# Prompt attention turned round: values as weights, turned probabilities moving

## The chip, the cores and the metric

The kernel runs on one core of a Trainium2 chip. The metric is device microseconds from the first to the last instruction of one launch; the median of several runs counts. TensorE multiplies (stationary weights, moving columns), VectorE and ScalarE work elementwise, GpSimd as well, SyncE starts the transfers. Each engine works through its own list in order, and they wait for each other by semaphores.

## What is computed

One layer of a hybrid decoder in fp32: 2064 prompt rows (16 meta and 2048 new) and 8 running sequences of 4 rows. Each layer runs sliding-window attention with sinks beside a gated delta recurrence, merges them by gates, and adds a feed-forward block. The change is in the attention of the prompt:

```
s = einsum('bnqkgd,bnskd->bnkgqs', qb, kband) * (HEAD_DIM ** -0.5)   # block of 128 queries, 256 keys
p = exp(s - m);  p = p / (sum(p) + exp(sink - m))
o = einsum('bnkgqs,bnskd->bnqkgd', p, vband)
h = h + (ga * (oa @ w_oa) + gb * (ob @ w_ob)) @ w_out
```

There are 8 query heads of 64 features, in two groups of four (GQ) for two key and value heads (NKV).

## The kernel before

The prompt is worked in four groups (NG) of four tiles (NT) of 128 rows; group 0 also carries the 48 small rows (16 meta, 32 of the running sequences), called tile "S". Each group runs through stages in written order: input projections (fp32r products, each weight split in a high and a low part: ScalarE casts `wh`, VectorE subtracts to get `wl`, L1628); the convolution blocks j = 0 to 11; the delta recurrence of one tile after another; the z blocks; the output projections; the feed-forward block. All these projections are issued by the helper at L724.

The attention of a tile is laid beside other work in steps. A table names for each part the step k at which every engine's list has it: `IN_CONV` for tile 0 of groups 1 to 3, whose steps are the convolution blocks, `IN_DELTA` for the next tile while the delta recurrence of this one runs, `IN_DELTA_S` beside tile "S". A part exists for both gk = 0 and 1, that is for the first and second four heads; 32 such rounds in all. A round is: scores on TensorE (L887, one head on each half of the rows), mask and maxima on VectorE (L1696, L1664 to L1667), exponentials on ScalarE (L1336), the turn of the 128 x 256 probabilities of four heads by eight transposes (L899), copies of the turned ones out of PSUM to `pTm` by ScalarE (L1350) and VectorE (L1681), and the products with the values (L912). `denominators` gives one over the sum of each row (L1672, L1673).

Within the delta stretch the steps are: k = 3 + 2q after TensorE's first product chain of level q (L1043) and the transposes to X (L1048), k = 4 + 2q after the second (L1056), for q = 0 to 4. L1043 waits for VectorE's Y pass (L1913), which waits for L1056; L1056 waits for ScalarE's copies PT and X (L1429, L1433). k = 13 follows the products L1063 and L1067. `QUARTERS` gives for each k how many quarters of a gate block (six products of 512 columns by L724) TensorE works there, ahead of the attention's part; after every fourth quarter ScalarE casts and VectorE splits the next weight, also ahead of the attention's part. That is at k = 2, 6, 12 and 17. GpSimd masks for level q (L1577) after the first product of level q - 2.

At the end of the attention the rows of `qkv` hold the output with tokens on the partitions. In the z stretch TensorE transposes them (L1138) into PSUM, ScalarE rounds them to `oT[0]`, VectorE takes the rest to `oT[1]` (L1982), and the output projection reads both.

Of the kernel before, what the change touches and what calls it, by code (L numbers as in the profile page):

```python
# [55 lines left out]
assert sum(QUARTERS) * NT == 64  # L56
IN_DELTA = dict(inputs=2, scores=(3, 8), exp=(5, 10), transposes=(6, 11), values=(7, 13))
IN_DELTA_S = dict(inputs=1, scores=(2, 6), exp=(3, 7), transposes=(4, 8), values=(5, 13))
# [23 lines left out]
for _v, _names in {  # L82
# [18 lines left out]
        (0, 4, 4):  # L101
            "oaT_ps ob_hi ob_lo prod_done z_silu",
        (0, 5, 4):
# [6 lines left out]
        (0, 8, 8):  # L110
            "hn_hi hn_lo hsq_done mix_f mix_hi mix_lo pT_rd0 sqc_done sum_ps ysq_done",
        (0, 9, 0):
# [139 lines left out]
def program(nc, d):  # L252
# [130 lines left out]
    for n in """hi_done lo_done unit_started const_in param_in ident_in x_in0 x_in1 x_in2 x_in3 x_inS xT_in rope_in conv_state_in  # L383
        hx_in hxS_in kv_out y_out end_out yS_out s_cache_in s_state_in s_mask_in v_meta_in
        act_step dve_step pool_step sq_done rr_done xR_ps xs_done xh_done xl_done a_ps a_rd ab_rd
        beta_done rope_done conv_ps conv_rd conv_y conv_post tail_done attT_ps att_in sc_ps sc_done pexp_done
        pT_ps pT_rd0 pT_rd1 pv_ps oa_done e_done att_m nat_ps G_ps arg_done dec_done natq_done bt_ps bt_rd kk_ps
        A_done QK_done X_done Y_ps Y_done m_done PT_ps PT_done X_ps X_rd DT_ps XY_done WU_ps WT_rd U_rd WS_ps u_done ob_rd
        QB_zero small_p o_ps dS_ps S_done osq_done orr_done ob_done gate_ps gate_e gate_done z_ps z_silu obT_ps ob_lo oaT_ps
        oT_hi oT_lo prod_done mix_ps mixS_ps mix_rd mix_f mix_hi mix_lo state_out act_g dve_g gate_eS act_pre  # L390
        ob_hi dve_S out_ps h_done hn_hi hn_lo hsq_done hacc_done hsum_ps hpre_done hrr_done hR_ps hR_done
        ff_ps_g ff_ps_u ga_done sg_done hu_done hf_done hid_hi hid_lo down_ps h2_done ysq_done yacc_done sqc_done sum_ps
        gc_ps gc_in sums_in rs_done eg_done ysumS_ps ypreS_done yrrS_done yRS_ps yS_done ysum_ps ypre_done yrr_done yR_ps y_done kwm_done masked_done""".split():
        sem(n)
# [228 lines left out]
    def group(g, first):  # L623
# [90 lines left out]
        def tensor(pe, claim):  # L714
# [176 lines left out]
            def att_transposes(t, gk):  # L891
                r = round_of(t, gk)
                pe.wait_ge(*made("pexp_done", r + 1))
                for q in range(2):
# [7 lines left out]
            def att_values(t, gk):  # L902
# [5 lines left out]
                claim(4, "oa_done", r + 1)  # L908
                for y in range(GQ):
                    ps = slice(HD * (y % NKV), HD * (y % NKV + 1))  # L910
                    for s in range(2):
                        last = nc.tensor.matmul(bank[4][:, HD * y:HD * (y + 1)], pTm[:, 2 * y + s, :], vn[:, s, ps],  # L912
                                                start=s == 0, stop=s == 1)
# [219 lines left out]
            for j in range(NH):  # L1133
                feature_block("z", j, (1, 0)[j % 2], 2, "z_ps", "z_silu", j + 1)
                b = (6, 7)[j % 2]
                claim(b, "oT_lo", (j + 1) * (1 + F))
                for t in range(NT):
                    last = nc.tensor.transpose(bank[b][:, P * t:P * (t + 1)], qkv[:, t + 1, P * j:P * (j + 1)], c("ident"))  # L1138
                last.then_inc(sem("oaT_ps"), 1)
                if j == 0:  # L1140
# [117 lines left out]
        def scalar(act):  # L1258
# [211 lines left out]
            for j in range(NH):  # L1470
# [6 lines left out]
                act.activation(sz[:, CA], bank[(1, 0)[j % 2]][:, 0:WA], ACT.Silu).then_inc(sem("z_silu"), 1)  # L1477
                act.wait_ge(*made("oaT_ps", j + 1))
                act.copy(oT[0][:, j, MAIN], bank[(6, 7)[j % 2]][:]).then_inc(sem("oT_hi"), 1)
                if first:  # L1480
# [125 lines left out]
        def vector(dve):  # L1606
# [68 lines left out]
            def attention_step(t, where, k):  # L1675
                for gk in range(NKV):
                    r = round_of(t, gk)
                    if k == where["transposes"][gk]:
                        denominators(r, GQ)
                        dve.wait_ge(*made("pT_ps", r + 1))  # L1680
                        v_.tensor_copy(pTm[:, 4:8, :], bank[2][:].rearrange("p (a n) -> p a n", a=4)).then_inc(sem("pT_rd1"), 1)  # L1681
                        settle()
                    if k == where["values"][gk]:
                        dve.wait_ge(*made("pv_ps", r + 1))
                        v_.tensor_tensor(qkv[:, t + 1, 256 * gk:256 * (gk + 1)].rearrange("p (a e) -> p a e", a=GQ),
                                         bank[4][:, 0:GQ * HD].rearrange("p (a e) -> p a e", a=GQ),
                                         bc(st[:, 20:20 + GQ], [P, GQ, HD]), ALU.mult).then_inc(sem("oa_done"), 1)
                    if k == where["scores"][gk]:
# [288 lines left out]
            for j in range(NH):  # L1977
                lo_until("z", j)
                dve.wait_ge(*made("oT_hi", (1 + F) * (j + 1)))
                if first:  # L1980
                    v_.tensor_tensor(oT[1][:, j, SM], qkv[:, 0, NS * j:NS * (j + 1)], oT[0][:, j, SM].bitcast(F32), ALU.subtract).then_inc(sem("oT_lo"), 1)
                v_.tensor_tensor(oT[1][:, j, MAIN], bank[(6, 7)[j % 2]][:], oT[0][:, j, MAIN].bitcast(F32), ALU.subtract).then_inc(sem("oT_lo"), 1)  # L1982
                dve.wait_ge(*made("z_silu", j + 1))
# [243 lines left out]
```

## Time and profile before

| | us |
|---|---|
| median of 3 runs (3611.22 to 3614.88) | 3612.71 |
| the profiled execution's own time | 3614.01 |
| its span | 3612.0 |
| TensorE busy (matmuls) | 3495.0 |
| VectorE busy | 1764.9 |
| ScalarE busy | 1290.5 |
| GpSimd busy | 305.7 |
| mean granted TensorE clock | 0.979 of full |

Busy time is the union of an engine's instructions. A fp32 product shows as two matmul instructions in the trace, a transpose as one. The start of a matmul row is when it enters; the rows merge instructions of one line that follow each other, with their number behind the x.

### The profile page before, as it was taken

The numbers are of one execution on the slowest core, as the hardware profiler recorded it, in microseconds if no ns is written. First come the engines' busy times: TensorE is split into PE (matmuls) and PEld (weight loads), VectorE is DVE, ScalarE is ACT, GpSimd is POOL, SyncE is SP. The second block draws the span as 40 slices with busy tenths as digits, with TensorE's granted clock in tenths as the row PEclk, the third lists the DMA queues.
The fourth block names the chain that finished last, engine by engine and source line by source line (L and its number), as shares of the span: only waits on it lengthen the run. The fifth ranks groups of instructions, "written<-read, shape, count | busy, mean of one in ns | idle before, by whom it ended". The sixth has DMA issues, their size and how long they took to land. (4 is left out here: it accounts for less than half of the span.)

```text
span 3612.0 us, 48790 instructions
## 1 busy us (share of the span) xinstructions
PE 3495.0 (97%) x19972; PEld 3032.7 (84%) x19972; DVE 1764.9 (49%) x3003; ACT 1290.5 (36%) x2302; POOL 305.7 (8%) x289
## 2 busy tenths in 40 slices
PE   7979999999999999999999999999999999999998
PEld 6868889999998888888878888888888888888886
DVE  3834334543436654554345744554344754454343
ACT  3313334321224544432224544432223544432222
POOL 2211110000003111000001211000000311000000
PEclk9969989999999999999999999999999999999999
DMA  4101102322233211333333211232324211233322
GB/s 170 60 19 53 32 24 71 105 86 87 88 129 106 63 36 42 105 100 94 94 134 119 71 37 42 71 117 96 97 90 164 80 38 36 68 109 103 95 93 85
DMA packets 88541, 298.63 MB, mean 83 GB/s; under 512 B 12272, under 2 KB 14272, under 8 KB 87536
## 3 DMA queue, kind: packets, MB, share of 16 engines
q1 hardware_dynamic: 88320, 295.51, 25.5%
q8 instruction: 160, 2.62, 0.3%
q14 instruction: 61, 0.50, 0.0%
HBM read 283.86 MB, written 12.62 MB: 82 GB/s over the span
## 5 line engine op out<-in xcount | busy, mean ns | idle before, releaser
L724 PE MATMUL bank<-hnT,wh 128*128 128x512 f32 (+1 forms) x3520 | 931.4, 352 | 0.0
L1628 DVE TENSOR_TENSOR wl<-raw,wh 128x1024 fp32r<-128x1024 f32 x480 | 594.7, 1239 | 642.8 <-ACT wh L1274 641.6
L724 PE MATMUL bank<-xnT,wh 128*128 128x512 f32 (+2 forms) x2560 | 736.6, 374 | 12.6 <-DVE d_dT L1879 9.9
L724 PEld LDWEIGHTS bank<-hnT,wh 128*128 128x128 f32 x3520 | 619.4, 188 | 91.4 <-issue 0.2
L1274 ACT CAST wh<-raw 128x1024 fp32r<-128x1024 f32 x480 | 500.5, 1043 | 391.3 <-PE bank L724 331.4
L724 PE MATMUL bank<-hnT,wl 128*128 128x512 f32 (+1 forms) x1760 | 622.2, 354 | 0.0
L724 PEld LDWEIGHTS bank<-xnT,wh 128*128 128x128 f32 x2560 | 448.7, 193 | 79.1 <-DVE d_dT L1879 11.2
L724 PE MATMUL bank<-hid,wh 128*128 128x512 f32 (+1 forms) x1760 | 468.3, 354 | 4.4 <-DVE wl L1628 3.2
L724 PE MATMUL bank<-xnT,wl 128*128 128x512 f32 (+2 forms) x1280 | 467.6, 366 | 0.0
L724 PEld LDWEIGHTS bank<-hnT,wl 128*128 128x128 f32 x1760 | 330.6, 188 | 45.8
L724 PEld LDWEIGHTS bank<-hid,wh 128*128 128x128 f32 x1760 | 309.6, 188 | 52.4 <-DVE wl L1628 5.2
L724 PE MATMUL bank<-hid,wl 128*128 128x512 f32 (+1 forms) x880 | 310.8, 353 | 0.0
L724 PEld LDWEIGHTS bank<-xnT,wl 128*128 128x128 f32 x1280 | 246.3, 192 | 39.8
L1519 ACT CAST hid<-hf 128x512 fp32r<-128x512 f32 (+1 forms) x88 | 55.5, 630 | 419.5 <-DVE hf L2080 419.5
L724 PEld LDWEIGHTS bank<-hid,wl 128*128 128x128 f32 x880 | 165.5, 188 | 23.9
L724 PE MATMUL bank<-oT,wh 128*128 128x512 f32 (+1 forms) x640 | 169.4, 353 | 4.4 <-DVE oT L1982 3.2
L724 PE MATMUL bank<-mixT,wh 128*128 128x512 f32 (+1 forms) x640 | 169.4, 352 | 1.9 <-DVE mixT L2012 1.9
L1516 ACT ACTIVATE sg<-sg 128x512 f32<-128x512 f32 (+1 forms) x88 | 56.5, 642 | 318.9 <-DVE sg L2068 318.9
L724 PE MATMUL bank<-wh,xnT 128*128 128x512 f32 (+1 forms) x544 | 138.1, 342 | 16.9 <-DVE wl L1628 16.9
L1577 POOL TENSOR_TENSOR d_m<-d_dA,cm 128x512 f32<-128x512 f32 (+1 forms) x83 | 119.8, 1451 | 364.1 <-PE bank L1043 214.2
L502 POOL TENSOR_SCALAR rr<-ss 128x1 f32<-128x1 f32 (+3 forms) x34 | 6.6, 193 | 1523.6 <-ACT xr L508 1028.9
L1913 DVE TENSOR_TENSOR Y<-Y,bank 128x512 f32<-128x512 f32 (+1 forms) x83 | 56.0, 675 | 161.2 <-PE bank L1056 161.2
(296 smaller groups left out, 4429.7 us busy)
## 6 DMA issues: line engine op xcount, KB each, us to landing
raw<-in_wstream SPq DMA_DIRECT2D x472, 512.0 KB, 3.5
xr<-in_x_prompt SPq DMA_DIRECT2D x16, 512.0 KB, 5.6
xT<-in_xT SPq DMA_DIRECT2D x4, 2048.0 KB, 12.0
hT<-in_xT SPq DMA_DIRECT2D x4, 2048.0 KB, 9.1
out_yp_out<-hT SPq DMA_DIRECT2D x16, 512.0 KB, 3.0
raw<-in_wstream SPq DMA_DIRECT2D x8, 528.0 KB, 3.3
Sb<-in_state_delta SPq DMA_DIRECT2D x1, 2048.0 KB, 10.4
out_ds_out<-Sb SPq DMA_DIRECT2D x1, 2048.0 KB, 6.3
```

The lines of the kernel that those rows point to most:

```text
L502: pool_link(pool, nc.gpsimd.tensor_scalar(dst, src, mul, EPS, ALU.mult, ALU.add))
L724: ins = nc.tensor.matmul(*a, **k)
L1274: act.copy(wh[n % HL][:, 0:m], raw[:, n % RAW, 0:m]).then_inc(sem("hi_done"), 1)
L1516: act.activation(sg[j % 2][:, live], sg[j % 2][:, live], ACT.Silu).then_inc(sem("sg_done"), 1)
L1519: act.copy(hid[0][:, jj, live], hf[j % 2][:, live]).then_inc(sem("hid_hi"), 1)
L1577: nc.gpsimd.tensor_tensor(q4[f"m{q % 2}"][0:n, :, 0:n], q4["dA"][0:n, :, 0:n], bh(c(f"lm{l}")[0:n, 0:n], [n, NH, n]), ALU.mult).then_inc(s ...
L1628: v_.tensor_tensor(wl[n % HL][:, 0:m], raw[:, n % RAW, 0:m], wh[n % HL][:, 0:m].bitcast(F32), ALU.subtract).then_inc(sem("lo_done"), 1)
L1913: v_.tensor_tensor(Y[0:n, :, 0:n], Y[0:n, :, 0:n], bank[3][0:n, 0:NH * n].rearrange("p (h n) -> p h n", h=NH), ALU.subtract).then_inc(sem( ...
```

## The change

The turn of the probabilities stays. The products with the values change sides: before, the turned probabilities of a head, one half of its keys at a time, are the weights and 64 columns of values move, eight products a round; after, the values of a kv head (64 columns) are the weights, and the turned probabilities of its two heads move, 256 columns, four products a round. The two kv heads write to the lower and upper half of the PSUM partitions, that is to the two halves of TensorE's columns. The output thus has features on its partitions. Its rows can then no longer be divided by their sums afterwards, so VectorE multiplies the probabilities (128 x 1024) by the reciprocals ahead of the turn, and TensorE's turn waits for that (`att_p`) and no longer for the exponentials. The transposes of the z stretch go away, ScalarE and VectorE read `qkv` there. In `IN_DELTA` the turn moves from steps 6 and 11 to 7 and 12, and the values of gk = 0 from 7 to 8. `IN_CONV` and `IN_DELTA_S` keep their steps.

```diff
-IN_DELTA = dict(inputs=2, scores=(3, 8), exp=(5, 10), transposes=(6, 11), values=(7, 13))
+IN_DELTA = dict(inputs=2, scores=(3, 8), exp=(5, 10), transposes=(7, 12), values=(8, 13))
             def att_transposes(t, gk):
                 r = round_of(t, gk)
-                pe.wait_ge(*made("pexp_done", r + 1))
+                pe.wait_ge(*made("att_p", 2 * t + gk + 1))
...
                 claim(4, "oa_done", r + 1)
-                for y in range(GQ):
-                    ps = slice(HD * (y % NKV), HD * (y % NKV + 1))
-                    for s in range(2):
-                        last = nc.tensor.matmul(bank[4][:, HD * y:HD * (y + 1)], pTm[:, 2 * y + s, :], vn[:, s, ps],
+                turned = pTm[:].rearrange("p (x y) n -> p x y n", x=2)
+                for s in range(2):
+                    for half in range(NKV):
+                        ps = slice(HD * half, HD * (half + 1))
+                        last = nc.tensor.matmul(bank[4][ps, 0:2 * P], vn[:, s, ps], turned[:, :, 2 * half + s, :],
                                                 start=s == 0, stop=s == 1)
...
                 feature_block("z", j, (1, 0)[j % 2], 2, "z_ps", "z_silu", j + 1)
-                b = (6, 7)[j % 2]
-                claim(b, "oT_lo", (j + 1) * (1 + F))
-                for t in range(NT):
-                    last = nc.tensor.transpose(bank[b][:, P * t:P * (t + 1)], qkv[:, t + 1, P * j:P * (j + 1)], c("ident"))
-                last.then_inc(sem("oaT_ps"), 1)
...
-                act.wait_ge(*made("oaT_ps", j + 1))
-                act.copy(oT[0][:, j, MAIN], bank[(6, 7)[j % 2]][:]).then_inc(sem("oT_hi"), 1)
+                if j == 0:
+                    act.wait_ge(*made("oa_done", round_of(NT - 1, NKV - 1) + 1))
+                act.copy(oT[0][:, j, MAIN].rearrange("p (t n) -> p t n", t=NT), qkv[:, 1:, P * j:P * (j + 1)]).then_inc(sem("oT_hi"), 1)
...
                         denominators(r, GQ)
+                        settle()
+                        v_.tensor_tensor(sc[:], sc[:], bc(st[:, 20:20 + GQ], [P, GQ, 2 * P]), ALU.mult).then_inc(sem("att_p"), 1)
                         dve.wait_ge(*made("pT_ps", r + 1))
...
                         dve.wait_ge(*made("pv_ps", r + 1))
-                        v_.tensor_tensor(qkv[:, t + 1, 256 * gk:256 * (gk + 1)].rearrange("p (a e) -> p a e", a=GQ),
-                                         bank[4][:, 0:GQ * HD].rearrange("p (a e) -> p a e", a=GQ),
-                                         bc(st[:, 20:20 + GQ], [P, GQ, HD]), ALU.mult).then_inc(sem("oa_done"), 1)
+                        v_.tensor_copy(qkv[:, t + 1, 2 * P * gk:2 * P * (gk + 1)], bank[4][:, 0:2 * P]).then_inc(sem("oa_done"), 1)
```

The order of TensorE in the delta stretch of the last group's third tile, from k = 9 to k = 13, before (`PT` and `X` are the recurrence's tiles, `sc` the probabilities, `pTm` the turned ones, `vn` the values, L724 on `xnT` the gate's quarters):

```order
L724 MATMUL bank0<-xnT0_80,wl1_78 128x512
L1043 MATMUL bank5<-Y_159,d_m0_153 128x128 [waits PT_done,XY_done,m_done]
L1048 MATMUL bank6<-cm_49,Y_159 128x128 [waits X_rd]
L899 MATMUL bank1<-cm_49,sc_116 128x128 [waits sc_done,pexp_done]
...
L1056 MATMUL bank3<-PT_160,X_158 128x128 [waits XY_done,X_rd,PT_done]
L724 MATMUL bank0<-xnT0_80,wh1_75 128x512
...
L1063 MATMUL bank5<-Y_159,d_kb_146 128x128 [waits PT_done,XY_done]
L1067 MATMUL bank6<-d_bv_148,Y_159 128x128 [waits X_rd]
L912 MATMUL bank4<-vn_54,pTm_117 128x64 [waits oa_done,pT_rd1,pT_rd0]
L1108 MATMUL bank1<-S_52,d_WQ_157 128x128 [waits S_done,pT_rd0,WT_rd]
```

The same place in the changed kernel (its lines behind the values are one higher):

```order
L724 MATMUL bank0<-xnT0_80,wl1_78 128x512
L1044 MATMUL bank5<-Y_159,d_m0_153 128x128 [waits PT_done,XY_done,m_done]
L1049 MATMUL bank6<-cm_49,Y_159 128x128 [waits X_rd]
L1057 MATMUL bank3<-PT_160,X_158 128x128 [waits XY_done,X_rd,PT_done]
L724 MATMUL bank0<-xnT0_80,wh1_75 128x512
...
L899 MATMUL bank1<-cm_49,sc_116 128x128 [waits sc_done,att_p]
...
L1064 MATMUL bank5<-Y_159,d_kb_146 128x128 [waits PT_done,XY_done]
L1068 MATMUL bank6<-d_bv_148,Y_159 128x128 [waits X_rd]
L913 MATMUL bank4<-pTm_117,vn_54 64x256 [waits oa_done,pT_rd1,pT_rd0]
L1109 MATMUL bank1<-S_52,d_WQ_157 128x128 [waits S_done,pT_rd0,WT_rd]
```

The turn stood between L1048 and L1056 and now stands behind the quarter that follows it.

VectorE's order at the same place, k = 11 to 13, before (`st` holds row sums and reciprocals, `wl` is the weight split):

```order
L1672 TENSOR_TENSOR st_68<-st_68 128x4 [waits pexp_done,dve_step,XY_done]
L1673 RECIPROCAL st_68<-st_68 128x4 [waits dve_step]
L1681 COPY pTm_117<-bank2 128x512 [waits pT_ps]
L1913 TENSOR_TENSOR Y_159<-Y_159,bank3 128x512 [waits Y_done,DT_ps,dve_step]
L1628 TENSOR_TENSOR wl0_77<-raw_73,wh0_74 128x1024 [waits hi_done,dve_step,XY_done]
L1685 TENSOR_TENSOR qkv_111<-bank4,st_68 128x256 [waits pv_ps]
```

And in the changed kernel (its lines stand one to three lower):

```order
L1910 TENSOR_TENSOR Y_159<-Y_159,bank3 128x512 [waits DT_ps,Y_done,dve_step,XY_done]
L1625 TENSOR_TENSOR wl0_77<-raw_73,wh0_74 128x1024 [waits hi_done,dve_step,XY_done]
L1669 TENSOR_TENSOR st_68<-st_68 128x4 [waits pexp_done]
L1670 RECIPROCAL st_68<-st_68 128x4 [waits dve_step]
L1678 TENSOR_TENSOR sc_116<-sc_116,st_68 128x1024 [waits dve_step]
L1680 COPY pTm_117<-bank2 128x512 [waits pT_ps]
L1684 COPY qkv_111<-bank4 128x256 [waits pv_ps,dve_step]
```

The reciprocals stood ahead of the Y pass and the weight split, and now stand behind both, with the multiplication of the probabilities after them.

VectorE's order at block j = 6 of the last group's convolution stretch in the changed kernel (`cy` are the taps):

```order
L1625 TENSOR_TENSOR wl2_79<-raw_73,wh2_76 128x1024 [waits hi_done]
L1824 COPY pre0_136<-tail_55 128x3 [waits conv_rd,conv_post]
L1825 COPY tail_55<-pre0_136 128x3 [waits dve_step]
L1768 TENSOR_SCALAR cy0_138<-pre0_136,pr_50 128x512
L1770 SCALAR_TENSOR_TENSOR cy0_138<-pre0_136,pr_50,cy0_138 128x512 [waits dve_step] x3
L1669 TENSOR_TENSOR st_68<-st_68 128x4 [waits pexp_done]
L1670 RECIPROCAL st_68<-st_68 128x4 [waits dve_step]
L1678 TENSOR_TENSOR sc_116<-sc_116,st_68 128x1024 [waits dve_step]
L1680 COPY pTm_117<-bank2 128x512 [waits pT_ps]
```

Nothing moved there; the multiplication is added behind the taps of the block, and TensorE's turn, which follows its own block j = 6, now waits for it.

## Rows read from the trace of the kernel before

**Rows 1.** The page, busy time and share of the span, instructions.

```profile
PE 3495.0 (97%) x19972; PEld 3032.7 (84%) x19972; DVE 1764.9 (49%) x3003; ACT 1290.5 (36%) x2302; POOL 305.7 (8%) x289
```

**Rows 2.** Timeline, TensorE, convolution stretch of group 3: start, us, line, operands.

```profile
2849.96 1.09 PE L899 MATMUL bank<-cm,sc 128*128 128x128 f32 x8
...
2856.42 0.95 PE L985 MATMUL bank<-cm,sqc 128*128 128x1 f32 x8
...
2866.68 1.07 PE L899 MATMUL bank<-cm,sc 128*128 128x128 f32 x8
```

**Rows 3.** Timeline, ScalarE's cast and VectorE, the same stretch.

```profile
2849.81 1.03 ACT L1274 CAST wh<-raw 128x1024 fp32r<-128x1024 f32 x1
...
2850.88 1.23 DVE L1628 TENSOR_TENSOR wl<-raw,wh 128x1024 fp32r<-128x1024 f32 x1 [3.18 <-ACT wh L1274]
...
2855.24 0.18 DVE L1673 RECIPROCAL st<-st 128x4 f32<-128x4 f32 x1
...
2857.31 0.17 DVE L1827 COPY pre<-tail 128x3 f32<-128x3 f32 x1 [0.18 <-ACT pre L1362]
...
2870.56 0.18 DVE L1673 RECIPROCAL st<-st 128x4 f32<-128x4 f32 x1
```

**Rows 4.** Timeline, TensorE (PEld: its weight loads), delta stretch of group 3.

```profile
3028.10 1.04 PE L899 MATMUL bank<-cm,sc 128*128 128x128 f32 x8
...
3031.68 1.89 PE L912 MATMUL bank<-vn,pTm 128*128 128x64 f32 x16
3033.41 1.11 PE L1056 MATMUL bank<-PT,X 128*128 128x128 f32 x8
3034.45 1.13 PE L887 MATMUL bank<-kT,qTt 64*128 64x256 f32 x8
3035.51 0.97 PEld L1043 LDWEIGHTS bank<-Y,d_m 128*128 128x128 f32 x8 [0.33 <-issue]
...
3040.61 1.05 PE L1043 MATMUL bank<-Y,d_m 128*128 128x128 f32 x8
...
3042.87 1.13 PE L1056 MATMUL bank<-PT,X 128*128 128x128 f32 x8
...
3045.23 1.05 PE L1063 MATMUL bank<-Y,d_kb 128*128 128x128 f32 x8
```

**Rows 5.** Timeline, VectorE, the same tile.

```profile
3028.39 1.22 DVE L1628 TENSOR_TENSOR wl<-raw,wh 128x1024 fp32r<-128x1024 f32 x1 [0.63 <-ACT wh L1274]
3029.72 0.18 DVE L1673 RECIPROCAL st<-st 128x4 f32<-128x4 f32 x1
...
3044.10 0.69 DVE L1913 TENSOR_TENSOR Y<-Y,bank 128x512 f32<-128x512 f32 x1 [0.40 <-PE bank L1056]
...
3044.82 1.23 DVE L1628 TENSOR_TENSOR wl<-raw,wh 128x1024 fp32r<-128x1024 f32 x1
```

**Rows 6.** Timeline, TensorE, the small rows' scores on column strips of 32.

```profile
110.73 0.65 PE L849 MATMUL bank<-kcT,QB 128*32 128x128 f32 x8
```

**Rows 7.** Timeline, VectorE's X pass of the last tile.

```profile
3069.60 1.67 DVE L1897 TENSOR_TENSOR X<-cm,X 128x512 f32<-128x512 f32 x1
```

**Rows 8.** GpSimd's mask products, whole run: min/median/max ns, first and last start.

```profile
L1577 POOL TENSOR_TENSOR d_m<-d_dA,cm x83: 591/1301/1800, 197.5 to 3084.9; 128x512 f32<-128x512 f32 x80, 48x192 f32<-48x192 f32 x3
```

**Rows 9.** Timeline, TensorE, delta stretch of the last tile, no attention beside it.

```profile
3093.39 1.05 PE L1043 MATMUL bank<-Y,d_m 128*128 128x128 f32 x8
...
3095.65 1.13 PE L1056 MATMUL bank<-PT,X 128*128 128x128 f32 x8 [0.77 <-ACT PT L1429]
```

**Rows 10.** TensorE's waits: us in total, times, longest.

```profile
PE bank L724 <- DVE oT L1982: 3.2, 3, 1.1
```

**Rows 11.** Stretches: length, busy PE, PEld, DVE, ACT, POOL, clock, DMA share, GB/s.

```profile
2891.00:2893.40 2.40, 0.23 (x2) 0.01 (x1) 2.33 (x6) 0.66 (x2) 0.00 (x0) 1.00 0.00 0
2893.40:2896.00 2.60, 2.60 (x13) 2.46 (x14) 0.55 (x1) 2.57 (x5) 0.00 (x0) 0.54 0.03 6
2896.00:2898.00 2.00, 2.00 (x14) 2.00 (x14) 0.78 (x3) 2.00 (x8) 0.00 (x0) 0.74 0.00 0
```

More of the change, by code:

```diff
@@ L101 @@
         (0, 4, 4):
-            "oaT_ps ob_hi ob_lo prod_done z_silu",
+            "ob_hi ob_lo prod_done z_silu",
         (0, 5, 4):
@@ L110 @@
         (0, 8, 8):
-            "hn_hi hn_lo hsq_done mix_f mix_hi mix_lo pT_rd0 sqc_done sum_ps ysq_done",
+            "att_p hn_hi hn_lo hsq_done mix_f mix_hi mix_lo pT_rd0 sqc_done sum_ps ysq_done",
         (0, 9, 0):
@@ L388, in program @@
         A_done QK_done X_done Y_ps Y_done m_done PT_ps PT_done X_ps X_rd DT_ps XY_done WU_ps WT_rd U_rd WS_ps u_done ob_rd
-        QB_zero small_p o_ps dS_ps S_done osq_done orr_done ob_done gate_ps gate_e gate_done z_ps z_silu obT_ps ob_lo oaT_ps
+        QB_zero small_p att_p o_ps dS_ps S_done osq_done orr_done ob_done gate_ps gate_e gate_done z_ps z_silu obT_ps ob_lo
         oT_hi oT_lo prod_done mix_ps mixS_ps mix_rd mix_f mix_hi mix_lo state_out act_g dve_g gate_eS act_pre
@@ L1981, in vector @@
                     v_.tensor_tensor(oT[1][:, j, SM], qkv[:, 0, NS * j:NS * (j + 1)], oT[0][:, j, SM].bitcast(F32), ALU.subtract).then_inc(sem("oT_lo"), 1)
-                v_.tensor_tensor(oT[1][:, j, MAIN], bank[(6, 7)[j % 2]][:], oT[0][:, j, MAIN].bitcast(F32), ALU.subtract).then_inc(sem("oT_lo"), 1)
+                v_.tensor_tensor(oT[1][:, j, MAIN].rearrange("p (t n) -> p t n", t=NT), qkv[:, 1:, P * j:P * (j + 1)],
+                                 oT[0][:, j, MAIN].bitcast(F32).rearrange("p (t n) -> p t n", t=NT), ALU.subtract).then_inc(sem("oT_lo"), 1)
                 dve.wait_ge(*made("z_silu", j + 1))
```

## The prediction

> **What bounds the kernel now.** I read the page first: TensorE is busy for 3495.0 us of the 3612.0 us span, so almost nothing can be given to it without lengthening the run, and what is taken off it shortens the run unless a wait takes its place [rows 1]. Next I read the timeline of the stretches that hold the change. In the convolution stretch of groups 1 to 3 the reader is to see that TensorE turns the probabilities at 2849.96 and 2866.68 with no idle time before it, straight behind a convolution block [rows 2]. VectorE is far behind it there: the reciprocal of that round ends at 2855.42 and that of the second at 2870.74 [rows 3]. Nobody minds now, since turned probabilities are not yet scaled. In the delta stretch each instruction of TensorE starts as the last one's slot ends, through both rounds [rows 4], while VectorE works in bursts a few us behind it [rows 5].
>
> **Rate of each operation.** Eight turns of 128 columns take 1.04 us, the last one 0.27 of it, so one starts every 0.11 us and the eight hold TensorE for 0.87 us [rows 4]. The 16 instructions of today's value products (two for each of eight) hold it from 3031.68 to 3033.41, 1.73 us [rows 4]. The new ones are four products of 256 columns, eight instructions. No row has just that form; two come near. The scores are also eight instructions of 256 columns, on row halves, and take 1.13 us [rows 4]: one starts every 0.11 us although each has twice the columns of a turn, so two halves run side by side. Column strips do so too: eight products of 128 columns on four strips of 32 columns, all 128 rows, took 0.65 us at half clock [rows 6], where a start every 0.22 us (the turns' rate at half clock) would need over 1.5. So I price the new values like the scores: a slot of 1.06 us. This holds a toll: weight loads behind the scores begin only at 3035.51, 0.33 us late with nothing awaited, and the slot in front of them (3033.41 to 3034.45) is 1.04 us where eight starts of 0.11 would be 0.87 [rows 4]; with 0.2 for the entry at places where none was paid, a round saves 1.73 - 1.06 = 0.67 us at gk = 0 and 0.48 at gk = 1. The bound on the other side: halves one after the other double the spacing, 7 x 0.22 + 0.38 = 1.9 us, which saves nothing.
>
> The Trainium skill speaks against the halves. TensorE: Matmul & The Clock Gate, Part 3, says that a weight load overlaps a product in flight only where the row groups differ, and two column halves have the same rows. By the strips' row the trace disagrees [rows 6], and I go by the row; by the rule the values would stay at some 1.8 us, and that is the third rival below.
>
> **The pass that is added.** VectorE now multiplies the 128 x 1024 probabilities, and TensorE's turn waits for that (att_p) and not for the exponentials. The nearest row with as many elements and both operands in SBUF is the weight split, 1.23 us [rows 5]; I take 1.22, and 0.07 for the semaphore.
>
> *Convolution stretch, groups 1 to 3.* At gk = 0 the chain is: last exponential, ScalarE's cast, weight split, the block's taps, sum, reciprocal, ending at 2855.42 [rows 3]; scaled at 2856.68, turned from 2856.75. TensorE would have gone at 2849.96 [rows 2]. Behind its waiting turn stand the next convolution block and all after it, so 6.8 us are lost. At gk = 1 VectorE's chain hangs on the end of the next block (the copy at 2857.31 waits for it), which moves along. From that block's end (2856.42) to the reciprocal's end are 14.32 us, plus 1.22, 0.04 and 0.07 makes 15.65; today the turn starts 10.26 after it [rows 2, 3]. That is 5.4 more. Minus 0.48 for the values: 11.7 us a group, **35 us** for three. The three groups run the same tables, so I count the one shown three times.
>
> *Delta stretch, gk = 0, turn moved from k = 6 to 7* (nine tiles in groups 1 to 3). Take the rows' tile. The product chain of k = 7 begins at 3028.10, where the turn was, so TensorE would turn at 3031.68 - 0.87 = 3030.81. VectorE ends the split at 3029.62 and the reciprocal at 3029.90 [rows 5]. GpSimd is in between: its mask product, 1.3 us [rows 8], is released by the end of that product chain (1.06 us long), and so asks at 3029.2. VectorE and GpSimd do not read and write together here: an X pass of 512 columns took 1.67 us beside it where the Y pass of that size takes 0.69 [rows 5, 7]. Which is first when the split ends no row shows; I let GpSimd win at 3029.6, to 3030.9; scaled at 3032.2, so TensorE waits 1.4 us. If VectorE wins, it waits 0.4. Less 0.67: **+0.73 us** a tile, bounds -0.3 and +1.1 (sum and reciprocal behind GpSimd too).
>
> *gk = 1, turn moved from k = 11 to 12.* Today the turn at k = 11 costs nothing. From L1043 at 3040.61 to L1056 at 3042.87 are 2.26 us with a turn between them; in the last tile, which has none, from 3093.39 to 3095.65 are 2.26 us too, with 0.77 of waiting for ScalarE's copies [rows 4, 9]. Moved, the turn leaves that wait behind and costs its full 0.87 at k = 12. There it waits also: VectorE passes Y (from 3044.10), then the split that k = 12 begins with (3044.82 to 3046.05), sum and reciprocal to 3046.4, scaling to 3047.7 [rows 5]. TensorE is ready at 3045.23, where L1063 starts [rows 4]: 2.5 us of waiting. Sum 0.87 + 2.5 - 0.48 = **+2.9 us**. A tile is 3.6, nine tiles **32 us**.
>
> *Group 0* holds the other eight rounds. Products of the 48 small rows stand around them or the clock is halved, so the waits are covered or the faster values weigh more; bounded by eight savings of 0.6 (-5) and eight waits of 0.9 net (+7) I take 0.
>
> *z stretch.* 64 turns go, at 0.11 each 7.0 us. The last four of each group were cover: TensorE waits there for oT already [rows 10], and the chain from z over ScalarE to VectorE is as long as before; 4 x 0.45 come back. **-5 us.** Copies and subtractions from SBUF cost their engines what they cost from PSUM and nobody waits for them longer.
>
> **The clock.** After TensorE stood for 2.2 us (busy 0.23 of 2.40) its granted clock was 0.54 and 0.74 of full in the next 2.6 and 2.0 us, the lower of its two levels for most of it [rows 11]: 2.6 x 0.46 + 2.0 x 0.26 = 1.7 us lost. Six waits of 5 to 7 us will each bring such a fall, at 1.7 to 3.4 us, I take 2.5: 15 us. The nine of 2.5 us are just beyond that row's; half of them at 1.7 is 7 us. **+22 us.**
>
> **Sum.** 35 + 32 + 0 - 5 + 22 = +84 us on the profiled execution's own 3614.0 us. The median of the runs shown is 1.3 us below it, so 3612.7 + 84 = 3697 us.
>
> **Rivals.** (a) *Everything hides, faster*: VectorE's scaled tile is there when TensorE comes. Then 32 values save some 0.57 each (18), z gives 5, and only the moved turns cost (9 x 0.87 = 8): 3598 us. It decides where VectorE reaches the round at least 1.6 us ahead of TensorE; against it stands that in the rows VectorE's reciprocal comes 5.5 and 4.1 us after the turn [rows 2, 3]. Chance 0.04. (b) *The waits come but the clock holds*: 3675 us. For it, most waits in the delta stretch are short; against it [rows 11]. Chance 0.2. (c) *The halves don't run side by side*: about 29 values that count cost 0.75 more, 22 us: 3719. Chance 0.12. (d) *The stage's order hides the waits of the delta stretch alone* (GpSimd never in the way and the split done early): 3697 - 32 - 7 = 3658. Chance 0.06. The forecast keeps 0.57, and 0.01 is left for no change.
>
> **Range.** From 3660, which takes in (b) with GpSimd losing the port, to 3728, which takes in (c) and falls of the clock at their upper price. Within 0.2% (7 us) of before is about what a measurement can't tell from no change. Only (a) is faster. Faster 0.04, same 0.01, slower 0.95.
>
> **What would show it.** In the profile after: TensorE's row of turns (L899) waits for VectorE's scaling in the convolution stretch of groups 1 to 3, near 6.8 and 5.4 us, six times; some 1.4 and 2.5 us in nine tiles; L1057 (L1056 today) waits some 0.8 us for ScalarE's copies in nine more places; the new values take about 1.1 us for eight instructions; the scaling takes 1.2 us; PEclk dips in the slices of the three convolution stretches. What would make me wrong: a scaling that is much faster or slower than the split, column halves in turn, or a clock that doesn't fall.

## The result and the profile after

The changed kernel takes 3696.13 us (median of 4 runs, 3692.91 to 3698.36), the kernel before 3612.41 beside it (4 runs, 3611.22 to 3614.88): ratio 1.0229, 95% interval 1.0213 to 1.0245. The change makes the kernel slower by 2.3%, and 3697 was forecast. The span of the profiled execution is 3696.4 us, 84.4 more than before.

The page's busy times and its row of granted clocks, to be held beside [rows 1]:

```profile
PE 3495.9 (95%) x19652; PEld 3005.1 (81%) x19652; DVE 1816.2 (49%) x3035; ACT 1290.7 (35%) x2302; POOL 307.7 (8%) x289
...
PEclk9869999999999999999999899999999999999999
```

TensorE has 320 instructions fewer and the same busy time: products ran at half clock. All that the span grew by is idle. VectorE's 51 us more are no reason in themselves, since it is half idle in either kernel. TensorE's waits show where its idle time is (us in total, times, longest):

```profile
PE bank L899 <- DVE sc L1678: 80.4, 26, 6.8
...
PE bank L1057 <- ACT PT L1425: 15.5, 21, 0.8
...
PE bank L724 <- DVE oT L1979: 6.3, 4, 1.7
```

Before, the turn waited for VectorE nowhere. The turns' rows on TensorE's timeline in group 3: the convolution stretch (first two), then the three delta tiles with attention beside them:

```profile
2911.23 1.97 PE L899 MATMUL bank<-cm,sc 128*128 128x128 f32 x8 [6.73 <-DVE sc L1678]
2936.11 1.97 PE L899 MATMUL bank<-cm,sc 128*128 128x128 f32 x8 [6.06 <-DVE sc L1678]
2989.77 1.09 PE L899 MATMUL bank<-cm,sc 128*128 128x128 f32 x8 [1.32 <-DVE sc L1678]
3006.02 1.97 PE L899 MATMUL bank<-cm,sc 128*128 128x128 f32 x8 [2.38 <-DVE sc L1678]
3051.87 1.09 PE L899 MATMUL bank<-cm,sc 128*128 128x128 f32 x8 [1.32 <-DVE sc L1678]
3068.50 1.09 PE L899 MATMUL bank<-cm,sc 128*128 128x128 f32 x8 [2.72 <-DVE sc L1678]
3112.75 1.09 PE L899 MATMUL bank<-cm,sc 128*128 128x128 f32 x8 [1.33 <-DVE sc L1678]
3129.01 1.97 PE L899 MATMUL bank<-cm,sc 128*128 128x128 f32 x8 [2.35 <-DVE sc L1678]
```

The same work that took 1.04 to 1.09 us takes 1.97 where the granted clock has fallen to the lower level. The stretch around the first wait, with the columns of [rows 11]:

```profile
2907.00:2910.00 3.00, 0.00 (x0) 0.00 (x0) 2.82 (x7) 1.38 (x3) 0.00 (x0) 0.50 0.58 178
2910.00:2914.00 4.00, 2.77 (x11) 2.58 (x12) 1.87 (x2) 0.77 (x2) 0.00 (x0) 0.50 0.00 0
2914.00:2917.00 3.00, 3.00 (x9) 2.32 (x8) 1.23 (x1) 0.77 (x1) 0.00 (x0) 0.50 0.00 0
```

VectorE at that place. Its taps (L1770) end at 2909.63; the sum, the reciprocal and the multiplication are queued behind them:

```profile
2907.30 2.33 DVE L1770 SCALAR_TENSOR_TENSOR cy<-pre,pr,cy 128x512 f32<-128x512 f32 x3
2909.55 0.15 DVE L1669 TENSOR_TENSOR st<-st 128x4 f32<-128x4 f32 x1
2909.74 0.18 DVE L1670 RECIPROCAL st<-st 128x4 f32<-128x4 f32 x1
2909.95 1.23 DVE L1678 TENSOR_TENSOR sc<-sc,st 128x1024 f32<-128x1024 f32 x1
```

**By stage.** To compare stages of two executions I take starts on TensorE's timeline: the first product of k = 13 in a delta tile (L1063, after it L1064) and the first output product that reads oT. The last tile's pair before, and then after:

```profile
3098.00 1.06 PE L1063 MATMUL bank<-Y,d_kb 128*128 128x128 f32 x8
...
3138.69 0.70 PE L724 MATMUL bank<-oT,wh 128*128 128x512 f32 x2 [1.06 <-DVE oT L1982]
```

```profile
3183.70 1.05 PE L1064 MATMUL bank<-Y,d_kb 128*128 128x128 f32 x8
...
3223.10 0.71 PE L724 MATMUL bank<-oT,wh 128*128 128x512 f32 x2 [1.53 <-DVE oT L1979]
```

The stretch between them is 40.69 us before and 39.40 after. The same subtraction for every group gives the table. The second row holds the stages of output, feed-forward, projections and convolution and one delta tile with attention; the third holds two such tiles and one without.

| stretch, groups 0 to 3 or 1 to 3 | before | after | difference |
|---|---|---|---|
| z stretch, groups 0 to 3 | 47.5, 40.7, 40.7, 40.7 | 46.2, 39.4, 39.4, 39.4 | -5.2 |
| first oT product to the first delta tile of the next group | 679.6, 623.7, 622.9 | 697.4, 644.9, 645.1 | +61.2 |
| three further delta tiles | 166.8, 166.4, 166.4 | 176.3, 175.6, 175.9 | +28.2 |
| start to the last delta tile of group 0 | 543.3 | 543.5 | +0.2 |

The sum is +84.4, the whole growth of the span. Six attention tiles cost 28.2, 4.7 each; with three more of them taken off the second row, 47 us are the convolution stretches'.

### The profile page after: what moved, and what is told of

Read it like the earlier page. It is cut to its first block and busy times, and to the rows that moved or that the text cites. A ratio compares the mean times of both kernels' runs of the same rounds, so it can differ in the third digit from the quotient of the medians.

```text
span 3696.4 us, 48182 instructions
## 1 busy us (share of the span) xinstructions
PE 3495.9 (95%) x19652; PEld 3005.1 (81%) x19652; DVE 1816.2 (49%) x3035; ACT 1290.7 (35%) x2302; POOL 307.7 (8%) x289
## 5 line engine op out<-in xcount | busy, mean ns | idle before, releaser
L724 PE MATMUL bank<-hnT,wh 128*128 128x512 f32 (+1 forms) x3520 | 931.4, 352 | 0.0
L724 PE MATMUL bank<-xnT,wh 128*128 128x512 f32 (+2 forms) x2560 | 745.2, 377 | 12.6 <-DVE d_dT L1876 9.9
L724 PEld LDWEIGHTS bank<-hnT,wh 128*128 128x128 f32 x3520 | 619.4, 188 | 91.4 <-issue 0.2
L724 PE MATMUL bank<-hnT,wl 128*128 128x512 f32 (+1 forms) x1760 | 622.2, 354 | 0.0
L724 PEld LDWEIGHTS bank<-xnT,wh 128*128 128x128 f32 x2560 | 455.5, 196 | 81.7 <-DVE d_dT L1876 11.2
L724 PE MATMUL bank<-xnT,wl 128*128 128x512 f32 (+2 forms) x1280 | 471.5, 369 | 0.0
L724 PE MATMUL bank<-hid,wh 128*128 128x512 f32 (+1 forms) x1760 | 468.1, 354 | 2.9 <-DVE wl L1625 2.7
L724 PEld LDWEIGHTS bank<-hnT,wl 128*128 128x128 f32 x1760 | 330.6, 188 | 45.8
L724 PEld LDWEIGHTS bank<-hid,wh 128*128 128x128 f32 x1760 | 309.6, 188 | 50.7 <-DVE wl L1625 4.4
L724 PE MATMUL bank<-hid,wl 128*128 128x512 f32 (+1 forms) x880 | 310.8, 353 | 0.0
L724 PEld LDWEIGHTS bank<-xnT,wl 128*128 128x128 f32 x1280 | 249.5, 195 | 40.4
L724 PEld LDWEIGHTS bank<-hid,wl 128*128 128x128 f32 x880 | 165.5, 188 | 24.0
L724 PE MATMUL bank<-oT,wh 128*128 128x512 f32 (+1 forms) x640 | 169.4, 353 | 6.3 <-DVE oT L1979 6.3
L724 PE MATMUL bank<-mixT,wh 128*128 128x512 f32 (+1 forms) x640 | 169.4, 352 | 1.9 <-DVE mixT L2010 1.9
L724 PE MATMUL bank<-wh,xnT 128*128 128x512 f32 (+1 forms) x544 | 139.2, 344 | 16.9 <-DVE wl L1625 16.9
```

The lines of the kernel that those rows point to most:

```text
L724: ins = nc.tensor.matmul(*a, **k)
```

## The experiments

All ratios are to the kernel before, run beside each experiment on the same chip; its medians there were 3613.1 to 3615.1 us. Differences in us between an experiment and the changed kernel are differences of ratios times 3613, and each ratio is known to some 0.0015, so such a difference is good to about 6 to 8 us; smaller ones need the stages.

**1. Without the multiplication.** A copy of one column stands in its place and the turn waits for the exponentials again; the attention's output stays undivided by its row sums.

```diff
-                        v_.tensor_tensor(sc[:], sc[:], bc(st[:, 20:20 + GQ], [P, GQ, 2 * P]), ALU.mult).then_inc(sem("att_p"), 1)
+                        v_.tensor_copy(st[:, 40:41], st[:, 16:17]).then_inc(sem("att_p"), 1)
...
-                pe.wait_ge(*made("att_p", 2 * t + gk + 1))
+                pe.wait_ge(*made("pexp_done", r + 1))
```

> The changed kernel without VectorE's multiplication; the turn waits for the exponentials again, as before the change (the attention output stays undivided by its row sums). My theory (the whole loss is that TensorE waits for VectorE's scaling, with the clock falls that follow): all waits of the turn go, the rest of the change is a gain: about 3597 us, at most 3604, with no wait over 1 us before a turn in groups 1 to 3. Rival (the moved turns or the new products themselves cost): it stays above the 3612 us of before, by up to 8 us for the turns that leave an idle place of 0.8 us behind.

It took 3596.48 us, ratio 0.9953 (0.9938 to 0.9968). The scaling with all that hangs on it is worth 100 us, and the rest of the change alone would be a gain of 17. TensorE's wait list has no row of L899 left, while the wait left behind by the moved turn stays as in the changed kernel:

```profile
PE bank L1057 <- ACT PT L1425: 15.5, 21, 0.8
```

**2. The old table.** The turn and values of the delta stretch at the steps of the kernel before:

```diff
-IN_DELTA = dict(inputs=2, scores=(3, 8), exp=(5, 10), transposes=(7, 12), values=(8, 13))
+IN_DELTA = dict(inputs=2, scores=(3, 8), exp=(5, 10), transposes=(6, 11), values=(7, 13))
```

> The changed kernel with the old steps (turns at 6 and 11, values at 7 and 13). My theory by the rows: at step 6 the turn waits 3.1 us (now 1.3 at step 7), at step 11 some 0.3 us and fills the wait for ScalarE's copies (now 2.35 + 0.77), so a tile gains about 1.1 us and nine tiles 10 us: 3686 us. Rival (the move of the steps was needed and hides waits): slower than the changed kernel's 3696, by up to 16 us if step 11 waits as long as step 12 does.

It took 3686.77 us, ratio 1.0206 (1.0189 to 1.0223). By the medians the moved table costs about 8 us; the intervals alone allow no more than that it does not help. The stages say more: three further tiles take 173.5, 171.9 and 173.9 us where the changed kernel has 176.3, 175.6 and 175.9, and that of experiment 4, with the steps of the changed one, 174.9 to 175.2. The move thus costs 0.9 to 1.4 us for each tile with attention. TensorE's timeline in the last such tile shows why: the turn of gk = 0 waits 2.95, that of gk = 1 not at all, and L1057 behind it does not wait either.

```profile
3101.17 1.10 PE L899 MATMUL bank<-cm,sc 128*128 128x128 f32 x8 [2.95 <-DVE sc L1678]
...
3116.39 1.09 PE L899 MATMUL bank<-cm,sc 128*128 128x128 f32 x8
3117.32 1.06 PE L1057 MATMUL bank<-PT,X 128*128 128x128 f32 x8
```

At k = 11 the reciprocal and the multiplication stand ahead of the Y pass and the split; moved to k = 12 they stand behind both, as the orders ahead of the prediction show.

**3. Both products on one column half.** The halves one after the other on the lower 64 columns; the features of the upper half are not computed.

```diff
-                for s in range(2):
-                    for half in range(NKV):
-                        ps = slice(HD * half, HD * (half + 1))
-                        last = nc.tensor.matmul(bank[4][ps, 0:2 * P], vn[:, s, ps], turned[:, :, 2 * half + s, :],
+                for half in range(NKV):
+                    ps = slice(HD * half, HD * (half + 1))
+                    for s in range(2):
+                        last = nc.tensor.matmul(bank[4][0:HD, 2 * P * half:2 * P * (half + 1)], vn[:, s, ps], turned[:, :, 2 * half + s, :],
```

> The changed kernel with both kv heads' products on the lower column half, one after the other (the upper half of the attention output isn't computed). My theory (column halves run side by side): the eight instructions take about 1.9 us and not 1.08, 27 rounds count, +24 us: 3720 us. Rival (weight loads don't overlap on halves with the same rows, so the halves never ran side by side; 1.08 us is what eight such instructions take anyway): no change, 3696.

It took 3717.71 us, ratio 1.0289 (1.0274 to 1.0305). TensorE's timeline: the eight instructions take 1.93 us, and their successor starts 1.86 after them.

```profile
3069.43 1.93 PE L913 MATMUL bank<-pTm,vn 128*64 128x256 f32 x8
3071.29 1.13 PE L887 MATMUL bank<-kT,qTt 64*128 64x256 f32 x8
```

In the changed kernel they hold it for 1.02:

```profile
3114.67 1.08 PE L913 MATMUL bank<-pTm,vn 128*64 128x256 f32 x8
3115.69 1.13 PE L887 MATMUL bank<-kT,qTt 64*128 64x256 f32 x8
```

So halves of the columns do run side by side. The Trainium skill (TensorE: Matmul & The Clock Gate, Part 3) ties the overlap of weight loads to different row groups. The prediction read from it that column halves would take turns; the same Part also lists a speedup for three column tiles side by side. All four products here have the same rows, and the measurement decides against that reading.

**4. Order of the halves.** The changed kernel's products with the loop over the halves outside:

```diff
-                for s in range(2):
-                    for half in range(NKV):
+                for half in range(NKV):
+                    for s in range(2):
```

> The changed kernel with the loop over the kv heads outside that over the key halves: both products of the lower column half come first, then both of the upper half, instead of by turns. If neighbours in order must lie on different column halves to overlap, and the queue looks only one ahead, two of four products run alone: the eight instructions of L913 take about 1.5 us instead of 1.1, and the time is some 12 us longer, 3708. If the column halves overlap whatever the order: 1.1 us and 3696.

It took 3694.87 us, ratio 1.0227 (1.0210 to 1.0244), and the eight take 1.09:

```profile
3065.86 1.09 PE L913 MATMUL bank<-pTm,vn 128*64 128x256 f32 x8
3066.88 1.16 PE L1109 MATMUL bank<-S,d_WQ 128*128 128x128 f32 x8
```

The products need not alternate between the halves to overlap. The rival of this run falls.

**5. TensorE kept busy through the waits.** 24 products of 512 columns with an unused result ahead of each of the six turns in the convolution stretches, so that the clock is changed and not the moment at which the scaled tile is there:

```diff
+                if t == 0 and not first:
+                    claim(7, "pT_ps", r + 1)
+                    for _ in range(24):
+                        nc.tensor.matmul(bank[7][:], xnT[0][:, 0, NS:NS + P], xnT[0][:, 1, MAIN], start=True, stop=True)
```

> The changed kernel with 24 unused products of 512 columns (5.5 us) on TensorE ahead of each of the six turns in the convolution stretches of groups 1 to 3, where it waits for 6.8 and 6.1 us anyway. My theory (the falls of the granted clock behind these waits cost 2 to 3 us each): the wait shrinks to about 1 us, the clock stays at its upper level there, and the time falls by about 14 us to 3682. Rival (the clock costs nothing there, only the wait does): 3696, and PEclk rises without effect.

It took 3682.8 us, ratio 1.0196 (1.0181 to 1.0211), some 12 to 13 us less than the changed kernel. TensorE's timeline in group 3, where the turn (here L903) comes 7.69 us after L990 as it came 7.68 after L986 in the changed kernel, but at full clock, and the stretch around it:

```profile
2894.28 0.95 PE L990 MATMUL bank<-cm,sqc 128*128 128x1 f32 x8
2895.09 5.84 PE L896 MATMUL bank<-xnT 128*128 128x512 f32 x24
2901.97 1.09 PE L903 MATMUL bank<-cm,sc 128*128 128x128 f32 x8 [1.04 <-DVE sc L1682]
```

```profile
2900.00:2905.00 5.00, 3.96 (x21) 3.03 (x21) 2.80 (x6) 1.53 (x2) 0.00 (x0) 1.00 0.04 15
```

These six falls are gone, but others with them, so the total alone does not give their price. In the delta tiles the clock falls in three places in place of six, though the waits there are as long as before. The turn that ran at half clock at 3006.02 in the changed kernel is here:

```profile
2991.62 1.09 PE L903 MATMUL bank<-cm,sc 128*128 128x128 f32 x8 [2.35 <-DVE sc L1682]
```

And at the start of each delta stretch, where the changed kernel has a fall and the kernel before has one in two of three groups ([rows 11]), this one has none. In group 3 the fall of the changed kernel is the first row, and the second is what TensorE waits for here:

```profile
2963.00:2969.00 6.00, 4.48 (x25) 4.22 (x25) 2.69 (x8) 5.10 (x12) 0.00 (x0) 0.72 0.01 3
```

```profile
2957.57 0.66 PE L1035 MATMUL bank<-cm,X 128*128 128x128 f32 x4 [1.47 <-DVE X L1898]
```

Where the clock falls at that place, this wait for VectorE's X is 0.2 us or none; where it doesn't, 1.5, in each of the kernels before, after and here. A fall there thus costs next to nothing.

By stage, of the two profiled executions: from the first turn of a convolution stretch to k = 13 of the first delta tile are 90.6 us in every group here, 94.5, 96.5 and 96.6 in the changed kernel, together 15.8 more. About 2 of them are falls in a delta tile (1.6 each, two of which begin just ahead of the mark) and 0.6 those at the start of the delta stretches. That leaves 13 us for the six falls behind the waits for the scaled tile, 2.2 each. The three falls that are gone from the delta tiles are worth 5 more, and 3 us came back where nothing was changed: 16.0 between these two executions, 12 to 13 by the ratios.

**6. The multiplication earlier in the delta stretch.** A hook at the head of a step on VectorE, ahead of the weight split; the turn of gk = 1 goes back to k = 11:

```diff
+IN_DELTA = dict(inputs=2, ..., transposes=(7, 11), values=(8, 13), scale=(6, 11), late=(-1, -1))
...
+            def attention_scale(t, where, k):
+                for gk in range(NKV):
+                    if k == where["scale"][gk]:
+                        denominators(round_of(t, gk), GQ)
+                        settle()
+                        v_.tensor_tensor(sc[:], sc[:], bc(st[:, 20:20 + GQ], [P, GQ, 2 * P]), ALU.mult).then_inc(sem("att_p"), 1)
...
             def beside(t, k):
+                if after(t) is not None:
+                    attention_scale(after(t), IN_DELTA_S if t == "S" else IN_DELTA, k)
```

> The changed kernel with the reciprocals and the multiplication of the probabilities moved one step ahead on VectorE in the delta stretch (k = 6 and 11, ahead of the weight split of that step), and the turn of gk = 1 at k = 11; the convolution stretch stays. Theory (the wait of the turn is the price, and it stands where VectorE reaches the multiplication too late): the waits of L899 of 1.3 and 2.3 us in nine tiles vanish, and so do most of the clock falls of the delta stretch; the hole of L1057 is filled again by the turn of gk = 1. 9 x 4.2 = 38 and some 8 of clock less: about 3650 us. Rival (VectorE's work is only shifted: the multiplication of 1.22 us now delays the weight split or the Y pass, on which TensorE waits instead): 3680 to 3697, with the waits of L724 or L1044 on VectorE up by what L899 loses.

It took 3639.01 us, ratio 1.0076 (1.0061 to 1.0091): 55 us gained where 46 were expected. By stage, the three further tiles of group 3 take 163.1 us, 12.8 less than in the changed kernel and even 3.3 less than before. A tile with attention is 1.7 us shorter than before; the faster values give 1.15 of it, and the runs do not show where the rest comes from. VectorE in the last tile with attention:

```profile
3055.57 1.23 DVE L1677 TENSOR_TENSOR sc<-sc,st 128x1024 f32<-128x1024 f32 x1
3056.71 2.32 DVE L1625 TENSOR_TENSOR wl<-raw,wh 128x1024 fp32r<-128x1024 f32 x1
3059.26 0.69 DVE L1688 COPY pTm<-bank 128x512 f32<-128x512 f32 x1 [0.22 <-PE bank L899]
...
3067.33 1.22 DVE L1677 TENSOR_TENSOR sc<-sc,st 128x1024 f32<-128x1024 f32 x1
```

```profile
3058.18 1.03 PE L899 MATMUL bank<-cm,sc 128*128 128x128 f32 x8
3059.05 1.06 PE L1057 MATMUL bank<-PT,X 128*128 128x128 f32 x8
```

The split has moved behind the multiplication and, beside GpSimd's mask product (from 3056.61), takes 2.32 us; no row of TensorE waits longer for it. The rival, that the pass only shifts the wait to the split or Y, falls.

**7. The multiplication earlier in the convolution stretch.** The same hook at the head of blocks j = 6 and 8, ahead of the weight split and the taps:

```diff
+IN_CONV = dict(inputs=4, scores=(5, 7), exp=(5, 7), transposes=(6, 8), values=(7, 9), scale=(6, 8), late=(-1, -1))
...
+                if not first:
+                    attention_scale(0, IN_CONV, j)
```

> The changed kernel with the multiplication at the head of blocks j = 6 and 8 on VectorE, ahead of the weight split and the taps of the block; the delta stretch stays. Theory (the six waits of 6.8 and 6.1 us are the taps and the split, queued ahead of the multiplication): they fall to under 2 us each, some 28 us less, and the six clock falls of the convolution stretch with them, another 13 to 16: about 3653 us. Rival (the weight split now comes late to the next block): waits of L724 on wl rise by 1.2 us a turn, so some 7 us come back: 3660 to 3665. Rival that the clock falls come from another cause than the wait: they stay, 3668.

It took 3655.72 us, ratio 1.0120 (1.0105 to 1.0135): 39 us gained. TensorE's turns in group 3:

```profile
2881.84 1.09 PE L899 MATMUL bank<-cm,sc 128*128 128x128 f32 x8 [1.62 <-DVE sc L1677]
2900.38 1.09 PE L899 MATMUL bank<-cm,sc 128*128 128x128 f32 x8 [0.96 <-DVE sc L1677]
```

and two stretches, behind the first and around the second:

```profile
2882.00:2886.00 4.00, 4.00 (x17) 3.31 (x17) 3.86 (x8) 3.51 (x5) 0.00 (x0) 0.64 0.38 133
...
2898.00:2902.00 4.00, 3.04 (x22) 2.74 (x21) 3.20 (x7) 3.97 (x8) 0.00 (x0) 1.00 0.00 0
```

The waits are nearly gone. The rival that the weight split would then come late to the next block falls: TensorE waits for `wl` 20.3 us where the changed kernel has 19.6, not the 7 more that it asked for. The clock still fell behind the wait of 1.62 us, in all three groups, and not behind that of 0.96, so not all of the clock's share came back. That fits the 4 us short of the expected 43, a shortfall that the ratios alone could not tell from none.

**8. Both moves.**

> Both moves together: all 24 multiplications of groups 1 to 3 and of the delta stretch ahead of the weight split of their step. If the waits and their clock falls are all of the price, the two gains add: 3696 - 45 - 43 = about 3608, near the kernel before (3613) or below it. If VectorE's added 1.22 us a round moves elsewhere: 3640 or more.

It took 3603.44 us (7 runs, 3600.93 to 3605.83), ratio 0.9972 (0.9961 to 0.9983): faster than the kernel before by 0.3%, and the gains add (55 and 39, together 93). What TensorE still waits for at the turns:

```profile
PE bank L899 <- DVE sc L1686: 8.4, 2, 4.3
PE bank L899 <- DVE sc L1677: 8.0, 6, 1.8
```

These are the two of tile "S", which I did not move, and six of the convolution stretch; they explain that 7 us are missing to the kernel without any multiplication. By stage this one is 9.4 us longer in the second row and 2.6 in group 0, and 5.4 shorter in the further delta tiles, where the other has the wait at L1057.

**9. The old value products.** The eight products of 64 columns in the changed kernel; the output then has its tokens on the partitions, so what the output projection reads is not the layer's attention.

```diff
+                for y in range(GQ):
+                    ps = slice(HD * (y % NKV), HD * (y % NKV + 1))
+                    for s in range(2):
+                        last = nc.tensor.matmul(bank[4][:, HD * y:HD * (y + 1)], pTm[:, 2 * y + s, :], vn[:, s, ps],
```

> The changed kernel with the eight products of 64 columns of the kernel before in place of the four of 256; all else is as in the changed kernel, and the output of the attention is then laid out with the tokens on the partitions, so the values that the output projection reads are not the layer's. Theory (the new products save 0.67 us in gk = 0 and 0.48 in gk = 1): 3696 + 16 x 0.67 + 16 x 0.48 = 3714 us, between 3709 and 3722. Rival (the new ones save nothing, because something else sets the time there): 3696.

It took 3714.18 us, ratio 1.0273 (1.0256 to 1.0290), 16 us more than the changed kernel. Turning the products round is a gain of 16 us, near the 18 that the slots gave.

**10. The z transposes back,** with their output unused:

```diff
+                b = (6, 7)[j % 2]
+                claim(b, "oT_lo", (j + 1) * (1 + F))
+                for t in range(NT):
+                    nc.tensor.transpose(bank[b][:, P * t:P * (t + 1)], qkv[:, t + 1, P * j:P * (j + 1)], c("ident"))
```

> The changed kernel with the sixteen transposes a group issued again in the z stretch into the same banks, their output unused. Theory: the transposes took 7.0 us of TensorE's path, of which 1.8 had hidden waits of the output projection for VectorE: 3696 + 5 = 3701 us. Rival (the waits for oT stay, since nothing reads the transposes): 3703. Rival that they were hidden: 3696.

It took 3706.85 us, ratio 1.0252 (1.0237 to 1.0268). The difference of 8 us can't tell 5 from 7, but the stage can. The pair that bounds it in the last group:

```profile
3192.18 1.06 PE L1064 MATMUL bank<-Y,d_kb 128*128 128x128 f32 x8
...
3232.91 0.70 PE L724 MATMUL bank<-oT,wh 128*128 128x512 f32 x2 [1.09 <-DVE oT L1983]
```

That is 40.73 us against 39.40; the four groups give 1.34, 1.32, 1.31 and 1.33, in all 5.3. The wait for oT falls from 1.53 to 1.09 here, so the transposes had covered a part of it: the theory's 5 holds, the rival's 7 does not. The other 3 to 5 us of this run lie outside the z stretch: in its profiled execution 3.3 of them in the second row of the stage table. In that same row the kernel of experiment 4, which differs from the changed one only in the order of four products, is 4.6 us shorter; so differences of this size come and go between executions, without the transposes.

## Why the prediction was right

**The bound.** TensorE had no slack, and its queue runs in order: what the turn waits for, everything behind it waits for. Shown by the table of stages: every us of the growth lies in stages with a turn.

**Convolution, 35 + 15 forecast, 47 measured.** In experiment 5, where the clock never falls in the second row of the table, that row is 46.8 us longer than before; less three delta tiles without their falls (3.4 each, below) that leaves 37 for the waits (forecast 35), and the six falls are the 13 us of that experiment. The first turn waits 6.73 where 6.8 was forecast. The second comes 15.62 us after the end of the block before it (2920.49 to 2936.11), forecast 15.65. Its wait shows as 6.06 and not 5.4, because the faster values lie ahead of it on the path and their 0.67 is part of this wait; the net stays 5.4. Group 1 lost 3 to 4 us less than the other two (+17.8 against +21.2 and +22.2). That is no property of the group: in experiment 4 the three read +18.6, +18.6 and +19.5.

**The delta stretch, 32 + 7 forecast, 42 measured.** A tile costs 4.7 where 3.6 and 0.8 of clock were forecast. In experiment 5 three of its falls are left in six tiles, which are 25.2 us longer than before; less 1.6 us for each fall, a tile costs 3.4. So the waits were sized a little high and the clock low. The waits are there: 1.32 to 1.33 (1.4) and 2.35 to 2.72 (2.5), and the wait list has twelve more rows of L1057 where I had foreseen nine (21 in place of 9, 9.3 us more): the three tiles of group 0 have the moved table too. GpSimd did win the port. VectorE and GpSimd at the turn of gk = 0:

```profile
3108.82 1.22 DVE L1625 TENSOR_TENSOR wl<-raw,wh 128x1024 fp32r<-128x1024 f32 x1 [0.63 <-ACT wh L1270]
3109.97 1.25 DVE L1669 TENSOR_TENSOR st<-st 128x4 f32<-128x4 f32 x1
```

```profile
3109.67 1.53 POOL L1574 TENSOR_TENSOR d_m<-d_dA,cm 128x512 f32<-128x512 f32 x1 [3.71 <-PE bank L1044]
```

A sum of four columns, 0.15 us elsewhere, took 1.25 and ended when GpSimd's product did. The Trainium skill (SBUF — State Buffer, SBUF: two separate sides) says that where a VectorE instruction has two SBUF inputs and GpSimd's reads SBUF, whichever of the two starts first has the shared port for its whole instruction; the trace agrees. That this wait came out at the forecast's size is in part luck. The prediction let the sum and the reciprocal pass ahead of GpSimd; they came behind it, which costs 0.25 us more. GpSimd was done 1.16 us after the split and not 1.3, and TensorE itself came 0.2 later.

**The clock, 22 forecast.** Six falls in the convolution stretches are 13 us by the stages of experiment 5 (forecast 15). In the delta stretch the clock fell in six places, such as the turn at 3129.01:

```profile
3129.00:3132.50 3.50, 3.48 (x18) 3.49 (x19) 0.69 (x1) 0.58 (x1) 0.00 (x0) 0.54 0.32 118
```

That is 3.5 x 0.46 = 1.6 us, 10 for six (forecast 7), and experiment 5, which lost three of them with the waits left as they were, agrees: 5 us for the three. Six of nine waits of 2.35 to 2.72 us brought a fall where half were forecast. The page was less use than I had said: a slice is 92 us wide, and of the three convolution stretches only the second shows a dip to 8.

**z and group 0.** -5 and 0 forecast, -5.2 and +0.2 measured. In z the prediction's sentence that copies from SBUF cost what they cost from PSUM holds to 0.03 us (ScalarE's 0.61 against 0.58, VectorE's 0.69 both). In group 0 no attention turn of a delta tile waits at all; the 0 was set between bounds and not worked out.

**The rivals.** (a) needed VectorE ahead of TensorE; it came as late as the rows said, and with the multiplication left out 3596 was measured where (a) put 3598. (b), a clock that holds, is refuted by the rows at 1.97. (c), halves one after the other, is experiment 3 and gives 3718, forecast 3719. Its row of column strips, [rows 6], holds eight instructions, which are four fp32 products and not eight; the comparison was by instruction and stands. (d) is refuted by the waits in all nine delta tiles with attention of groups 1 to 3.

What I had not seen: the price was not that of the multiplication but of its place. Of the 6.7 us of the first wait 5.1 were time in which VectorE worked off the split and the taps, though the exponentials were ready when TensorE came (1.62 are left in experiment 7); queued ahead of them, the same pass costs little, and the change becomes a small gain.

## What to carry to other kernels

When a pass is put between two engines, ask first what stands ahead of it in its engine's queue, and only then how long it lasts: here 1.2 us of work made TensorE wait up to 6.8 at one place and 1.6 or nothing at another. A turn or product moved later to give a producer time must not pass behind further work of that same producer, and it may have been the filler of another wait. Cost a change on a full TensorE by its waits and the clock after them, not by busy time: VectorE's busy time was alike in the slow version and in the one that wins.

## What the runs showed of the hardware

- Two 64-column halves with the same 128 rows run at the same time in fp32, whatever their order: 1.08 us for four products of 256 columns, 1.93 on one half.
- The clock does not follow from the length of the wait alone: after 2.38 and 2.35 us of waiting the turn ran at half clock (3006.02, 3129.01), after 2.72 at full (3068.50); in experiment 5 the turn of 3006.02 ran at full after 2.35. In experiment 7 the clock fell behind a wait of 1.62 in all three groups, in experiment 8 behind 1.62 in two, and behind 1.83 in the third it did not.
- Beside a GpSimd product VectorE's weight split took 2.32 us in place of 1.22, and a pass over four columns 1.25 in place of 0.15.
